# A transformer block on one core: vector loads on another queue, quarter projections between the turns of the probabilities, and another order of the last expert's round

## What is computed

```python
h = rms_norm(x, g_mix)
z = h @ w_in + b_in                     # 1024 x 5376: a, b, q, k, v, two gates
u = a * sigmoid(b)
u = depthwise_causal_conv(u, conv_w) + conv_b          # 31 taps, 1024 channels
y_conv = silu(layer_norm(u)) @ w_conv_out + b_conv_out
p = softmax_with_sinks(q @ k.T * scale - slopes * dist)   # 16 heads, window of 128
y_attn = (p @ v) @ w_attn_out + b_attn_out
x = x + (sigmoid(gate_conv) * y_conv + sigmoid(gate_attn) * y_attn) @ w_out
hf = rms_norm(x, g_ffn)
w, e = top4(softmax(hf @ w_router + b_router))         # of 32 experts
for every expert: y += w * (((up + 1) * gate * sigmoid(1.702 * gate)) @ w_down + b_down)
out = rms_norm(x + y, g_final)
```

## Time and profile before

| | |
|---|---|
| timed runs, median | 1176.87 us |
| profiled execution | 1177.35 us |
| its span | 1175.6 us |
| PE busy | 1123.7 us (96%) |
| DVE, ACT, POOL busy | 326.1, 179.6, 47.6 us |
| loaded | 440 MB, mean 376 GB/s over the span |
| mean granted TensorE clock | 0.996 of full |

### The profile page before, as it was taken

One profiled execution on the slowest core, in us unless ns is written; L12 is line 12 of the kernel. 1 busy time (PEld: TensorE's weight loads), 2 busy tenths in 40 slices (PEclk: granted clock), 3 DMA queues, 4 the chain that ended last, 5 costly groups with the idle time before them and its releaser, 6 DMA issues.

```text
span 1175.6 us, 13690 instructions
## 1 busy us (share of the span) xinstructions
PE 1123.7 (96%) x5333; PEld 532.8 (45%) x5333; DVE 326.1 (28%) x793; ACT 179.6 (15%) x351; POOL 47.6 (4%) x39
## 2 busy tenths in 40 slices
PE   8999799999999999999999999999999999999997
PEld 7888687865333333333333333333333333333332
DVE  1899964224111111111111121121111111111111
ACT  2111266123011010010010110010000000000011
POOL 2560000000000000000000000000000000000000
PEclk9999999999999999999999999999999999999999
DMA  8966416659999999999999999999999999999996
GB/s 267 349 219 179 143 72 251 250 215 333 423 423 428 434 430 431 431 431 433 430 433 431 433 431 430 433 431 433 431 431 431 434 431 430 431 431 435 433 423 259
DMA packets 54134, 441.69 MB, mean 376 GB/s; under 512 B 4184, under 2 KB 34138, under 8 KB 37337
## 3 DMA queue, kind: packets, MB, share of 16 engines
q1 hardware_dynamic: 53512, 440.20, 90.4%
q0 software_dynamic: 432, 0.95, 0.4%
q10 hardware_dynamic: 160, 0.13, 0.0%
HBM read 440.08 MB, written 1.05 MB: 375 GB/s over the span
## 4 chain that ended last, share of the span: by engine, by line
PE 82%; DVE 6%; DMA 4%; issue 4%; another core or an unknown queue 2%; DVEq 1%; ACT 0%; ACTq 0%
PE bank L1447 54%; PE bank L1193 8%; PE bank L1415 5%; DVE arena L822 4%; PE bank L1400 4%; DMA arena<-in_w_down 4%; PE bank L1311 2%; PE bank L1483 2%; PE bank L1454 1%; PE bank L1407 1%; PE bank L1490 1%; DVEq L821 1%; PE bank L1343 1%; PE bank L1216 1%
## 5 line engine op out<-in xcount | busy, mean ns | idle before, releaser
L1447 PE MATMUL bank<-arena,x_columns 128*64 128x512 f32 x2080 | 467.7, 594 | 21.1 <-DMA arena<-in_w_up 19.7
L1447 PEld LDWEIGHTS bank<-arena,x_columns 128*64 128x64 f32 x2080 | 149.7, 137 | 293.4 <-issue 272.7
L1447 PE MATMUL bank<-arena,act_columns 128*64 128x512 f32 x992 | 219.1, 593 | 9.3 <-DMA arena<-in_w_down 9.3
L1193 PE MATMUL bank<-arena 128*128 128x256 f32 x928 | 204.2, 381 | 1.1 <-DVE arena L789 1.1
L1193 PEld LDWEIGHTS bank<-arena 128*128 128x128 f32 x928 | 175.8, 191 | 27.0 <-issue 1.8
L1447 PEld LDWEIGHTS bank<-arena,act_columns 128*64 128x64 f32 x992 | 76.4, 137 | 148.2 <-issue 148.2
L822 DVE SCALAR_TENSOR_TENSOR arena<-arena x240 | 97.3, 484 | 0.1
L1047 DVE TENSOR_SCALAR bias_selector<-ones_bf,expert_onehot 96x64 bf16<-96x64 bf16 x32 | 7.6, 237 | 268.7 <-PE bank L1407 268.7
L1081 DVE TENSOR_SCALAR gate_clipped<-bank 128x512 f32<-128x512 f32 x32 | 22.1, 692 | 202.7 <-PE bank L1447 202.7
L1085 DVE TENSOR_SCALAR hidden<-bank 128x512 f32<-128x512 f32 x32 | 22.1, 691 | 181.6 <-PE bank L1447 181.6
L1415 PE MATMUL bank<-y_block,scatter 64*128 64x512 f32 x248 | 61.5, 614 | 0.0
(11 more groups left out here) (192 smaller groups left out, 498.6 us busy)
## 6 DMA issues: line engine op xcount, KB each, us to landing
arena<-in_w_up SPq DMA_DIRECT2D x25, 4096.0 KB, 44.7
arena<-in_w_down SPq DMA_DIRECT2D x25, 4096.0 KB, 45.9
arena<-in_w_gate SPq DMA_DIRECT2D x24, 4096.0 KB, 43.5
arena<-in_w_in SPq DMA_DIRECT2D x21, 1024.0 KB, 11.8
arena<-in_w_gate SPq DMA_DIRECT2D x10, 2048.0 KB, 12.1
arena<-in_w_up SPq DMA_DIRECT2D x9, 2048.0 KB, 11.6
arena<-in_w_down SPq DMA_DIRECT2D x8, 2048.0 KB, 15.2
arena<-in_w_down SPq DMA_DIRECT2D x11, 1024.0 KB, 8.6
```

The costliest lines, as they stand in the source:

```text
L1193: last = pe.matmul(bank[n % 3][:, j * T:(j + 1) * T], w[:, c, j * P:(j + 1) * P], src[:, c, :], start=(c == 0), stop=(c == C - 1))
L1447: last = pe.matmul(dst[h * CAP:(h + 1) * CAP, :], lhs(row), cols(rows[:, row, :], h), start=(row == 0), stop=(row == MROWS - 1))
```

## The change

It has five parts.

1. **Vectors.** Seven vector loads and the conv taps are issued by ScalarE, behind its copies of the rows of 1 / rms, the router's weights behind its next wait; before, SyncE issued them behind piece 1 of w_in. TensorE turns the vectors after piece 0 (before: in the middle of piece 1) and the taps after piece 1 (before: after piece 2).
2. **Start.** TensorE makes the rows of 1 / rms between the transposes: row 0 after the first half of x, row 1 in the middle of the second. VectorE waits for x's second half by halves.
3. **Quarters.** For groups 0, 2 and 3 a quarter of a projection (4 products) stands before the third part of `turn_probs` and another behind it; before, the three parts stood together with half a projection behind them. Group 1 stays.
4. **Last round.** Matrix NM-3 (93) is now down 30 and NM-2 (94) up 31. The order is gate 31, down 30, up 31, the whole scatter of 30, turn_act, turn_weights, down 31, last scatter. The extra buffers and the half scatters go. Matrix 94 is loaded in four parts, 95 in five.
5. **Final norm.** The mean of the first half's squares plus eps becomes the bias of the root (`mean_of_half`), the root is taken directly behind the second square, and only one quarter (t = 1, h = 1) is still made in two steps.

```diff
-    if n == NM - 1:
-        return NE - 1, 2
+    if n >= NM - 3:
+        return ((NE - 2, 2), (NE - 1, 1), (NE - 1, 2))[n - (NM - 3)]
...
-ROW_PARTS[NM - 1] = [(0, 4), (4, 6), (6, 7), (7, 8)]
+ROW_PARTS[NM - 2] = [(0, 4), (4, 6), (6, 7), (7, 8)]
+ROW_PARTS[NM - 1] = [(0, 2), (2, 4), (4, 6), (6, 7), (7, 8)]
...
@@ SyncE @@
                 fetch(n, by_cols(n), w_in[:, :, col:col + COLS])
-                if n == 1:
-                    for name, (row, rows) in VEC.items():
-                        if name != "g_mix":
-                            sp.dma_start(vrows[row:row + rows, :],
-                                         t_in[name].rearrange("(c p) -> c p", p=P)).then_inc(vecs_loaded, 16)
-                    sp.dma_start(cwrows, t_in["conv_w"]).then_inc(cw_loaded, 16)
-                    sp.dma_start(wrt, t_in["w_router"].rearrange("(c p) e -> p c e", p=P)).then_inc(wrt_loaded, 16)
...
@@ ScalarE @@
+            for name, (row, rows) in VEC.items():
+                if name != "g_mix":
+                    act.dma_start(vrows[row:row + rows, :], t_in[name].rearrange("(c p) -> c p", p=P)).then_inc(vecs_loaded, 16)
+            act.dma_start(cwrows, t_in["conv_w"]).then_inc(cw_loaded, 16)
+
             act.wait_ge(vecs_out, 2)
+            act.dma_start(wrt, t_in["w_router"].rearrange("(c p) e -> p c e", p=P)).then_inc(wrt_loaded, 16)
...
             def y_std(t):
+
                 act.wait_ge(squares_dve, t + 1)
-                act.activation(std[:, 0, t:t + 1], ss[:, 1, t:t + 1], ACT.Sqrt, scale=1.0 / D,
-                               bias=eps[:, 0:1]).then_inc(stds, 1)
+                act.wait_ge(squares, TT + 2 * t + 2)
+                act.activation(std[:, 0, t:t + 1], ss[:, 3, t:t + 1], ACT.Sqrt, scale=1.0 / D,
+                               bias=ss[:, 1, t:t + 1]).then_inc(stds, 1)
 
             square(0, 0)
             square(0, 1)
+            y_std(0)
             square(1, 0)
-            y_std(0)
-            act.wait_ge(gain_on, 2)
+            act.wait_ge(gain_on, 1)
             square(1, 1)
             y_std(1)
...
@@ VectorE @@
-            dv.wait_ge(xTp, TT)
             dv.wait_ge(row_out, TT)
             for c in range(C):
+                if c % (C // 2) == 0:
+                    dv.wait_ge(xTp, 2 + c // (C // 2))
...
-            dv.wait_ge(squares, TT + 1)
-            gained(0, 0)
-            sum_of_squares(0)
+            mean_of_half(0)
             dv.wait_ge(y_done, 2 * TT)
             gained(1, 1)
             y_rstd(0)
-            dv.wait_ge(rstd_ready, 1)
-            dv.wait_ge(gain_on, 1)
-            dv.tensor_scalar(ysum[:, 0, 0:512], ysum[:, 0, 0:512], rstd[:, 0, 0:1], None, ALU.mult).then_inc(ysum_ready, 1)
+            half_out(0, 0)
+            mean_of_half(1)
             half_out(0, 1)
-            sum_of_squares(1)
             y_rstd(1)
             half_out(1, 0)
...
@@ TensorE @@
+            x_columns(0, range(C))
+            pe.wait_ge(gmix_loaded, 16)
+            pe.transpose(bank[1][:, 0:C], vrows[0:C, :], ident[0:C, 0:C]).then_inc(gmixT, 1)
+            rstd_to_row(0)
+            x_columns(1, range(C // 2))
+            rstd_to_row(1)
+            x_columns(1, range(C // 2, C))
...
             pe.wait_ge(cw_out, 1)
             pe.wait_ge(v_out, 1)
-            turn_probs(0)
-            project(GATE0 + 6, hT, (0,))
+            turn_probs(0, (0, 1))
+            project(GATE0 + 6, hT, (0,), chunks=FIRST)
+            turn_probs(0, (2,))
+            project(GATE0 + 6, hT, (0,), chunks=REST)
             sum_over_partitions(1, 2, ln_var)
             attend(0)
...
             gate_product(b, NM - 4)
+            down_product(b - 1, NM - 3)
             pe.wait_ge(swT_out, b)
-            up_product(NM - 3)
-            down_product(b - 1, NM - 2, dst=G, halves=(0,))
+            up_product(NM - 2)
+            pe.wait_ge(n_ready, 1)
+            n_blocks = pe.value_load(nblk_i[0:1, 0:1], min_val=NE, max_val=NBLK)
+            pe.wait_ge(yb_out, b)
+            scatter()
             turn_act(b)
             turn_weights(b)
-            down_product(b - 1, NM - 2, dst=G, halves=(1,))
-            pe.wait_ge(yb_out, b)
-            scatter((0,), swT_late, y_late)
-            down_product(b, NM - 1, columns=act_late)
-            scatter((1,), swT_late, y_late)
-            pe.wait_ge(n_ready, 1)
-            n_blocks = pe.value_load(nblk_i[0:1, 0:1], min_val=NE, max_val=NBLK)
+            down_product(b, NM - 1)
```

73 lines of the change are left out of this document (35 added, 38 removed).

## The result

The change took 1172.75 us in the median of seven executions, the kernel before 1176.87 us: ratio 0.9943, 95% interval 0.9919 to 0.9967 (that of the two medians alone is 0.9965, near the upper end of the interval). The kernel is faster, by 4.1 us of the medians instead of the 9.4 to 9.8 us predicted, and the median lies 0.75 us above the upper end of the range given, 1172 us. The median hides the more telling part.

| executions of the change | us | mean granted clock |
|---|---|---|
| two | 1167.54, 1168.58 | 0.998, 0.999 |
| three | 1172.74, 1172.75, 1172.90 | 0.995 |
| two | 1174.91, 1175.73 | 0.995 |

What follows compares the result with a forecast made beforehand. The stream of expert weights sets the end and ends earlier only if work before about 290 us moves forward. Terms -6.2 - 2.8 + 0.0 - 0.4 - 0.4 = -9.8 us take 1177.35 to 1167.5 us, range 1165 to 1172.

Steps and rivals of the forecast that it cites:

- the stand: TensorE's 5.80 us idle before the first sum over partitions, waiting for VectorE's reduction; said to shrink to about zero.
- the new wait of group 3: TensorE ahead of group 3's turns: the later third turn of group 2 brings a wait of 1.2 us.
- -6.2: Sum over partitions starts at 137.24 instead of 143.44 us; start and wait for vectors are contained.
- -2.8: Sum, scores and projection behind the stand run at the higher clock: -2.8 us, bounds 0 and -2.9.
- the start: First projection: four transposes fewer ahead of it, 0.9 us off, at 9.34 us; bound 0 if first weights land only then.
- the wait for vectors: TensorE behind the first projection waits for vector loads now on ScalarE's queue: 0.5 us taken, bounds 0 and 3.
- the clock: Without the stand TensorE's clock stays up behind it: -2.8 us; bound 0 if something else lets it fall.
- The rival of held issues: Seven vector loads on ScalarE's queue each held 3.06 us, TensorE stands 17.8 us: 1187.6 us, chance 0.10.
- Quarters: Quarter projections between the turns: -0.54 + 0.9 - 0.31 = 0.0 us, bounds -1.2 and +1.5.
- Last round and norm: At the end: new order leaves 1.1 us of waits instead of 1.5, -0.4 us; shorter VectorE norm chain, -0.4 us.
- The stream follows: Expert weights: a microsecond gained before about 290 us moves the stream, and the end, by a microsecond.
- Rival 3: A load before 290 us is bound by the DMA engines, so the shift is lost: 1176.5 us, chance 0.05.

Runs made afterwards that it cites:

- e2: The change without its quarters (groups 0, 2 and 3 turned in one piece again): 1168.17 us in the median.
- e4: The change with 9 unused products in the router's last stage and the four products that start y split two by two: 1170.05 us.
- e8: The change with 4 unused products in the router's last stage, y's start split and group 2 turned in one piece: 1167.40 us, ratio 0.9915.
- e6: The kernel before with 24 unused products in TensorE's idle time before the first sum over partitions: 1181.13 us, ratio 1.0017.
- e7: The change with the vector loads and conv taps back on SyncE's queue, the router's weights still on ScalarE's: 1171.96 us.
- e11: The change with 4 unused products in the router's stage, y's start split, group 2 in one piece, but old last round and norm: 1168.41 us.
- e1: The kernel before with the new last round and new final norm alone: 1176.77 us beside 1177.61 us for before, ratio 0.9996.
- e5: The change with 9 unused products ahead of the first w_attn_out projection, where TensorE is busy anyway, y's start in one piece: 1174.61 us.
- e12: e8 with 12 unused products before x's transposes and 3 between the last transpose and the first projection: 1168.84 us.

## Why the prediction was right, and where it was not

- **The time: off.** The median, 1172.75 us, is 5.2 us above the forecast and 0.75 above its range. The two undisturbed executions, 1167.54 and 1168.58 us, are the forecast of 1167.5.
- **Sign and mechanism at the stand: right.** The stand is gone. The sum stands at 137.66 us in e2, 137.14 in e4 and 137.17 in e8, where the text had 137.24; between the five traces with the old start and the five with the new one and none or little of the slow start it moved by 5.9 us in the mean (6.2 said). The vectors' transpose is at 16.66 to 16.91 us in e2, e4 and e8 (said: 16 to 17), the taps' at 24.0 to 24.5 (24.2), the new wait of group 3 is 1.19 us (1.2). The undisturbed level is met because the two large terms, -6.2 and -2.8, came nearly as priced. Inside the first, two errors cancel in part: the start brought 0.2 us instead of 0.9, and the wait for vectors, taken as 0.5, didn't come.
- **The step that failed** is the clock: "Without the stand the clock should stay up ... Bounds 0 (something else lets it fall) and -2.9." The -2.8 us behind the stand were there (from the sum to w_out 2.76 us less in e2, 2.66 in e6). The bound of 0 was wrong: the fall that comes instead is worse than the one that goes. In the change's profiled execution it costs 1.67 + 1.55 us in the router's stage and 1.69 us behind y's start on TensorE. The whole loss is larger: from the first gather to the last gate product the shift drops from 7.1 to 0.58 us, 6.5 us, where that of e2 drops by 0.7 us. The slow products are 4.9 of it; the other 1.6 us are lost further on in the stream, and no run takes them apart. And by the mean clocks falls came in five executions of seven. The text didn't look for other places that could let the clock fall, though the rows of the router's stage, waits between small products, stood in the trace of before.
- **The start: off.** The taken 0.9 us was 0.04 in the profiled execution (10.20 for 10.24 us) and 0.56 in e2. Most of the latter is chance: the first projection starts at 9.58 to 10.35 us in the five traces with the old start (mean 10.03), at 9.68 to 10.20 in the seven with the new one and no unused products there (mean 9.85), so the edit is worth 0.2 us if anything. The bound of 0 named the cause in most of them, the landing of the first weights. What no term had is the lower level in the first projection, 9.19 us for 7.14; it makes 2.0 us in the profiled execution. The change and e7 have it, e11 in small (7.61 us), and none of the five traces with the old start; whether the new start brings it isn't settled.
- **The vectors: right**, TensorE waits for none of them in any trace; the 0.5 us taken, above the text's own 0 to 0.4, was too much. Only the taps are waited for, 0.67 us in e2 and 0.15 in e4. The Trainium skill's rule (DMA: Bandwidth & Descriptors, Issuing engines are not separate DMA queues) that another issuing engine saves only issuing agrees with e7: 1166.65 to 1174.93 us with the loads on SyncE's queue, 1167.54 to 1175.73 on ScalarE's. The rival of held issues is out: on ScalarE's queue b_in took 0.65 us and the others some 0.3 us each.
- **Quarters: 0.0 said, -0.4 us measured** (e2). Group 2 costs the 0.9 us said (0.88 in e8); groups 0 and 3 gave 1.3 us together instead of 0.85, each 0.2 us more than its wait, for a reason that isn't known.
- **Last round and norm: 0.4 + 0.4 us said,** 0.6 + 0.57 by the trace of the change, 1.1 in e1's, nothing in e8 against e11. The waits left are 1.17 us, the text had 1.1; the rest of the round's gain, 0.25 us, lies in the products, which no term had. What the text priced at nothing, that the new order asks for the last weights sooner, shows in e4, e5, e8 and e12 as the wait for up 31, 0.3 to 0.9 us.
- **The stream follows**: right. Rival 3 is out by e2 and e8.

What stays open is why, by the mean clocks, a kernel with a fall at the stand has no later one in 49 of 57 executions, while with the stand filled they come in ten of twelve. The router's stage is the same code in both. It wasn't found which property of the stage counts, nor whether the unused products would do without the split of y's start.

## What to carry to other kernels

Where an edit removes a long wait of TensorE, look along its timeline for the next stretches of waits and small products, and price a fall of the clock there, before counting the gain; a spread of the times in groups, with a mean clock to each group, is the sign of it. A few unused products in such a stretch, in number what the waits hold, cost 0.16 us here, and 0.3 more with the split of y's start that went with them; together they brought 4 to 7 us in the executions concerned. Ahead of that, see whether the wait one removes pays for something else.

## What the runs showed of the hardware that was not expected

- The clock fell with TensorE almost always busy. In the change's trace, behind four products with 32 rows of weights, 3.69 us without a pause, it was 0.50. The same four products are not followed by a fall in before, e1, e2 and e5. Split in two by two around other products (e4, e8 to e12) they are followed by none in six traces, and the mean clocks of the 47 executions (0.998 or more, 0.996 where the stand is left) give no sign of one.
- One and the same kernel ran in groups of times 4.2 us apart and more from execution to execution (the change: 1167.54 to 1175.73 us). Before is steadier, but not free of it: of its 57 executions beside the experiments 49 lie between 1176.12 and 1180.99 us, the others at lower clocks and up to 1183.55.
- Filling a stand of 5.8 us with unused work made the kernel slower, 1181.13 against 1178.17 us for before beside it (e6).
- At the start the level can be low while the table of stretches gives a granted clock of 1.00; there only the pace of the products shows it (4 product records from 13 to 14 us, 7 from 15 to 16).
